# The norm's factor per token left out of the second block's operand and given to the results, with the operand turned during the down projection

## What is computed

```python
def hybrid_layer(x, cos, sin, norm_g, w_in, gate_bias, conv_w, ...):
    h = rms_norm_2(x, norm_g)              # x * rsqrt(mean(x^2) + eps) per token, times g per channel
    proj = jnp.einsum('bsd,dn->bsn', h, w_in)
    (q_a, k_a, v_a, o_a, i_a, f_a, z_a, c_q, c_kv, k_r, z_b, g_a, g_b) = jnp.split(proj, offsets, axis=-1)
    qk_a = jax.nn.silu(causal_depthwise_conv(jnp.concatenate([q_a, k_a], axis=-1), conv_w))
    q_a, k_a = jnp.split(qk_a, 2, axis=-1)
    h_a = mlstm_chunkwise(q_a, k_a, v_a, i_a + gate_bias[:H_A], f_a + gate_bias[H_A:])
    y_a = einsum(sigmoid(o_a) * rms_norm_2(h_a, mlstm_norm_g) * silu(z_a), w_a)
    q_b  = einsum(rms_norm_2(c_q, q_lat_g), w_uq)
    kv_b = einsum(rms_norm_2(c_kv, kv_lat_g), w_ukv)
    ...                                     # head norms, rotation of k_r and of part of q_b, causal attention o_b
    y_b = einsum(o_b * silu(z_b), w_b)
    return x + einsum(sigmoid(g_a) * y_a + sigmoid(g_b) * y_b, w_out)
```

## Time and profile before

| | |
|---|---|
| median of 3 runs | 2552.49 us (2551.92 to 2555.49) |
| the profiled execution's own time | 2552.33 us |
| its span in the trace | 2550.3 us |
| PE busy | 2511.5 us, 98% |
| PEld busy | 2131.9 us, 84% |
| DVE busy | 1619.7 us, 64% |
| ACT busy | 1251.4 us, 49% |
| POOL busy | 143.7 us, 6% |
| mean rate from memory | 200 GB/s |

### The profile page before, as it was taken

How to read it: one execution, slowest core, us unless ns; L and a number is a source line. 1 busy time by engine, 2 the same in 40 slices (tenths; PEclk the granted TensorE clock), 3 DMA queues, 4 the chain that set the end, 5 groups by cost and what they waited for, 6 DMA issues and landing times.

```text
span 2550.3 us, 34507 instructions
## 1 busy us (share of the span) xinstructions
PE 2511.5 (98%) x13608; PEld 2131.9 (84%) x13608; DVE 1619.7 (64%) x2365; ACT 1251.4 (49%) x1899; POOL 143.7 (6%) x148
## 2 busy tenths in 40 slices
PE   6999999999999999999999999999999999999999
PEld 2689899998888888888888888988888888888887
DVE  3566787786588886566665666665555554545554
ACT  3244433334465554355554555555566665544443
POOL 1001100000001110001110000001000000000000
PEclk9999999999999999999999999999999999999999
DMA  9953777775569885566665455555554555555555
GB/s 335 333 182 112 233 245 249 244 240 183 206 193 273 266 261 191 193 189 189 191 189 192 163 169 174 174 170 184 174 164 150 157 166 189 181 190 183 189 189 165
DMA packets 459104, 511.42 MB, mean 201 GB/s; under 512 B 36771, under 2 KB 327682, under 8 KB 458432
## 3 DMA queue, kind: packets, MB, share of 16 engines
q1 hardware_dynamic: 455936, 501.11, 62.0%
q0 software_dynamic: 2864, 8.11, 1.0%
q10 hardware_dynamic: 144, 0.02, 0.0%
HBM read 506.93 MB, written 2.22 MB: 200 GB/s over the span
## 4 chain that ended last, share of the span: by engine, by line
PE 94%; ACT 2%; DVE 2%; SPq 1%; issue 1%; DMA 0%; DVEq 0%; ACTq 0%
PE PG L926 17%; PE PG L928 17%; PE PG L927 17%; PE PG L916 13%; PE PG L919 6%; PE PG L935 4%; PE PG L937 4%; PE PG L936 4%; PE PS L1040 1%; SPq L746 1%; PE PS L831 1%; ACT wh L1179 1%; PE PG L847 1%; PE PS L1104 1%; PE PG L849 1%
## 5 line engine op out<-in xcount | busy, mean ns | idle before, releaser
L1576 DVE TENSOR_TENSOR wl<-raw,wh 128x1024 fp32r<-128x1024 f32 (+1 forms) x745 | 911.3, 1227 | 702.7 <-ACT wh L1179 701.0
L1179 ACT ACTIVATE wh<-raw 128x1024 fp32r<-128x1024 f32 (+1 forms) x745 | 786.7, 1058 | 860.7 <-PE PG L928 574.8
L916 PE MATMUL PG<-FHL,wh 128*128 128x512 f32 x1376 | 430.8, 396 | 2.4 <-DVE UP L1832 1.5
L926 PE MATMUL PG<-wh,HHL 128*128 128x512 f32 x832 | 331.2, 398 | 0.1
L928 PE MATMUL PG<-wl,HHL 128*128 128x512 f32 x832 | 324.8, 390 | 0.0
L927 PE MATMUL PG<-wh,HHL 128*128 128x512 f32 x832 | 324.1, 390 | 0.0
L919 PEld LDWEIGHTS PG<-FHL,wl 128*128 128x128 f32 x1376 | 256.2, 188 | 59.6
L919 PE MATMUL PG<-FHL,wl 128*128 128x256 f32 x1376 | 267.9, 278 | 0.0
L916 PEld LDWEIGHTS PG<-FHL,wh 128*128 128x128 f32 x1376 | 210.8, 189 | 5.2 <-issue 3.7
L928 PEld LDWEIGHTS PG<-wl,HHL 128*128 128x128 f32 x832 | 156.1, 188 | 33.6
L927 PEld LDWEIGHTS PG<-wh,HHL 128*128 128x128 f32 x832 | 156.5, 188 | 30.7
(11 more groups left out here) (402 smaller groups left out, 4213.0 us busy)
## 6 DMA issues: line engine op xcount, KB each, us to landing
raw<-in_w_in SPq DMA_DIRECT2D x208, 512.0 KB, 3.4
raw<-in_w_up SPq DMA_DIRECT2D x344, 256.0 KB, 3.4
raw<-in_w_ada SPq DMA_DIRECT2D x128, 512.0 KB, 5.0
raw<-in_w_down SPq DMA_DIRECT2D x84, 512.0 KB, 3.6
raw<-in_w_qkv SPq DMA_DIRECT2D x80, 512.0 KB, 4.4
first<-in_w_ada SPq DMA_DIRECT2D x78, 256.0 KB, 6.7
...
```

The source lines that it names most:

```text
L916: pe.matmul(to, hi[:, 128 * j:128 * j + 128], flat(FHL[:, step.k, :, :]), start=step.first, stop=False, skip_group_check=True)
L926: pe.matmul(dst, xh[:, cols], hi, start=step.first and j % per == 0, stop=False, skip_group_check=True)
L1179: ac.activation(wh[n % NSPL][:, 0:src.shape[1]], src, ACT.Copy).then_inc(S["hi"], 1)
L1576: dv.tensor_tensor(wl[n % NSPL][:, 0:x], src, wh[n % NSPL][:, 0:x], ALU.subtract).then_inc(S["lo"], 1)
```

## The change

The operand `HHL` of the second block is now made of XT, the residual itself, times g2; the factor per token `xr` is left out and multiplied into each product's result. With that, no transpose has to wait for the norm:

- `warm` and `scale` are gone for "h". The groups i = 0 to 5 of `turned` stand in `down1` (group i in column group i//2 + 1, at steps 5 and 8), groups 6 and 7 at steps 3 and 6 of lat.
- `norm` for "h" stands at step 1 of lat. A new job `rows_h` makes the factor also as rows: at step 2 DVE multiplies the identity with xr (DIAGH), at step 4 PE multiplies a matrix of ones with DIAGH, which gives the factor of each token in every partition, and at step 5 ACT copies that to RR.
- Results with tokens on the partitions get `scale=xr` in the ACT instruction that reads them. A scale column holds for 128 tokens, so what was one instruction of 128x1024 becomes two of 128x512 (mv_out, sig, silu, out, mix, mixb). lat's squares get xr too, and `lr` is multiplied by it.
- Results with tokens along the row are multiplied by RR on DVE: KRF and the two gate rows from small (the bias comes in two further instructions, and ACT's copy to KRF is gone), and all of mqk by a new instruction per product, MSG = PG times RR, 128x1024, at step 0 of the mv product. ACT's centre tap and DVE's other taps read MSG.
- Apart from this, the pair g = 1 of the first block's attention gets other steps for some of its pieces.

```diff
@@ -307,7 +307,7 @@
...
         if g == 1:
-            after, plus = ("k", 2, 0), ((14, 15, 16, 17, 18, 19, 25, 25, 26, 26), (27, 27, 28, 28, 29, 30, 32, 32, 33, 34))
+            after, plus = ("k", 2, 0), ((14, 15, 16, 17, 18, 19, 27, 27, 29, 29), (27, 28, 29, 29, 30, 31, 33, 33, 34, 35))
         if g == 7:
...
@@ -361,8 +361,13 @@
...
-    normed("h", ("tail2", 0, 0), ("lat", 0, 0))
+    P.put(("lat", 0, 0), 1, "norm", "h", 0)
+    for phase, n in enumerate((2, 4, 5)):
+        P.put(("lat", 0, 0), n, "rows_h", 0, phase, phase == 1)
+    for i in range(8):
+        turned("xh", i, ("down1", i // 2 + 1, 0) if i < 6 else ("lat", 0, 0), (5 if i < 6 else 3) + 3 * (i % 2))
...
@@ -375,6 +380,7 @@
...
     for g in range(4):
+        P.put(("mv", g, 0), 0, "m_conv", g, 6)
         P.put(("mv", g, 0), 0, "m_conv", g, 0)
...
@@ -581,6 +587,10 @@
...
+    DIAGH = at("DIAGH", [128, 2, 128], F32, 178)
+    RR = at("RR", [128, T], F32, 179)
+    MSG = [at(f"MSG{i}", [128, 4, T], F32, 140 + 4 * i) for i in range(2)]
...
@@ -606,7 +616,7 @@
...
-        return emptied(u + k) if k < 2 else emptied(u)
+        return emptied(u + k) if z == "f" and k < 2 else emptied(u)
...
@@ -690,7 +700,7 @@
...
-             "xf": (HN["f"], FHL[:, :, :, :].rearrange("p k a t -> p a k t"), "f", A1[:, 0, :]), "xh": (HN["h"], HHL, "h", g2)}
+             "xf": (HN["f"], FHL[:, :, :, :].rearrange("p k a t -> p a k t"), "f", A1[:, 0, :]), "xh": (XT, HHL, "h", g2)}
...
@@ -1004,13 +1014,17 @@
...
-                p = P.of["up" if key == "f" else "lat", 0]
+                p = P.of["up", 0]
...
+            elif (job, phase) == ("rows_h", 1):
+                w.wait_ge(S["diag_h"], 1)
+                w.wait_ge(*free(u))
+                pe.matmul(ps[:, 0:T], ones[:, :], flat(DIAGH[:, :, :]), start=True, stop=True).then_inc(S["side"], 1)
...
@@ -1087,13 +1101,15 @@
...
-                elif name in ("xf", "xh"):
+                elif name == "xf":
...
-                        w.wait_ge(S[f"scaled{n}"], nth("scale", (name[1], i), 0))
+                        w.wait_ge(S[f"scaled{n}"], nth("scale", ("f", i), 0))
+                elif name == "xh":
+                    w.wait_ge(S["res"], 2 * nth("res", ("down1", i // 2), 0))
...
-                apart = name in ("xf", "xh") and i == 0
+                apart = name == "xf" and i == 0
...
@@ -1324,9 +1340,10 @@
...
-            elif (job, phase) == ("small", 0):
-                w.wait_ge(*product_done("small", 0))
-                ac.activation(KRF[:, :], result("small", 0)[0:64, 0, 0:T], ACT.Copy).then_inc(S["kr_raw"], 1)
+            elif (job, phase) == ("rows_h", 2):
+                u = use("rows_h", 0, 1)
+                w.wait_ge(*full(u))
+                ac.activation(RR[:, :], bank(u)[:, 0:T], ACT.Copy).then_inc(emptying(u), 1)
...
@@ -1344,10 +1361,11 @@
...
                 w.wait_ge(*product_done("lat", key))
+                w.wait_ge(S["xr"], 2)
                 if key == 1:
...
                 for n in range(2):
-                    end = ac.activation(LJUNK[:, n, :], result("lat", key)[:, n, :], ACT.Square,
+                    end = ac.activation(LJUNK[:, n, :], result("lat", key)[:, n, :], ACT.Square, scale=xr[:, n:n + 1],
                                         accum_out=lss[:, 2 * key + n:2 * key + n + 1])
...
@@ -1360,23 +1378,24 @@
...
-                w.wait_ge(*product_done("mqk", g))
+                w.wait_ge(*out_done("mqk", g))
...
-                    end = ac.activation(MQK[b][:, j, :], result("mqk", g)[:, j // 2, T * (j % 2):T * (j % 2) + T],
-                                        ACT.Identity, scale=cw2[:, 3, ch:ch + 1])
+                    end = ac.activation(MQK[b][:, j, :], MSG[b][:, j, :], ACT.Identity, scale=cw2[:, 3, ch:ch + 1])
...
-                w.wait_ge(*out_done("mqk", key))
+                w.wait_ge(S["m_taps"], key + 1)
...
-                ac.activation(MV[key % 2][:, :, :, 0:T], result("mv", key)[:, :, :].rearrange("p j (h e) -> p j h e", h=2),
-                              ACT.Copy).then_inc(out_sem("mv", key), 1)
+                for n in range(2):
+                    end = ac.activation(MV[key % 2][:, n, :, 0:T], result("mv", key)[:, n, :].rearrange("p (h e) -> p h e", h=2),
+                                        ACT.Copy, scale=xr[:, n:n + 1])
+                end.then_inc(out_sem("mv", key), 1)
...
@@ -1406,15 +1425,19 @@
...
                     w.wait_ge(S["gated"], n - 1)
-                ac.activation(RG[n % 2][:, :, :], result(name, g)[:, :, :],
-                              ACT.Sigmoid if name == "sig" else ACT.Silu).then_inc(out_sem(name, g), 1)
+                for j in range(2):
+                    end = ac.activation(RG[n % 2][:, j, :], result(name, g)[:, j, :],
+                                        ACT.Sigmoid if name == "sig" else ACT.Silu, scale=xr[:, j:j + 1])
+                end.then_inc(out_sem(name, g), 1)
             elif (job, phase) == ("mix", 0):
...
                     w.wait_ge(*full(use("turned", ("ha", 7), 0)))
-                ac.activation(cols4(GA if name == "mix" else GB, g), result(name, g)[:, :, :],
-                              ACT.Sigmoid).then_inc(out_sem(name, g), 1)
+                for j in range(2):
+                    end = ac.activation(cols4(GA if name == "mix" else GB, g)[:, j, :], result(name, g)[:, j, :],
+                                        ACT.Sigmoid, scale=xr[:, j:j + 1])
+                end.then_inc(out_sem(name, g), 1)
             elif (job, phase) == ("qr_out", 0):
...
@@ -1892,10 +1914,26 @@
...
-                dv.tensor_scalar(gates[:, 0, :], ps[64:72, 0, 0:T], gb[:, 0:1], None, ALU.add)
-                w.wait_ge(S["kr_raw"], 1)
-                dv.tensor_scalar(gates[:, 1, :], ps[96:104, 0, 0:T], gb[:, 1:2], None,
-                                 ALU.add).then_inc(out_sem("small", 0), 1)
+                w.wait_ge(*product_done("small", 0))
+                w.wait_ge(*emptied(use("rows_h", 0, 1)))
+                dv.tensor_tensor(KRF[:, :], ps[0:64, 0, 0:T], RR[0:64, :], ALU.mult).then_inc(S["kr_raw"], 1)
+                dv.tensor_tensor(gates[:, 0, :], ps[64:72, 0, 0:T], RR[64:72, :], ALU.mult)
+                dv.tensor_tensor(gates[:, 1, :], ps[96:104, 0, 0:T], RR[96:104, :], ALU.mult).then_inc(c.sem, c.up())
+                w.wait_ge(c.sem, c.n)
+                dv.tensor_scalar(gates[:, 0, :], gates[:, 0, :], gb[:, 0:1], None, ALU.add)
+                dv.tensor_scalar(gates[:, 1, :], gates[:, 1, :], gb[:, 1:2], None, ALU.add).then_inc(out_sem("small", 0), 1)
+            elif (job, phase) == ("rows_h", 0):
+                w.wait_ge(S["xr"], 2)
+                dv.tensor_tensor(DIAGH[:, :, :], ident[:, :].unsqueeze(1).to_broadcast([128, 2, 128]),
+                                 xr[:, :].unsqueeze(2).to_broadcast([128, 2, 128]), ALU.mult).then_inc(S["diag_h"], 1)
+            elif (job, phase) == ("m_conv", 6):
+                g, b = key, key % 2
+                w.wait_ge(*product_done("mqk", g))
+                w.wait_ge(*emptied(use("rows_h", 0, 1)))
+                if g >= 2:
+                    w.wait_ge(S["m_centre"], g - 1)
+                dv.tensor_tensor(MSG[b][:, :, :], result("mqk", g)[:, :, :].rearrange("p a (c n) -> p (a c) n", c=2),
+                                 RR[:, :].unsqueeze(1).to_broadcast([128, 4, T]), ALU.mult).then_inc(out_sem("mqk", g), 1)
...
@@ -1933,18 +1971,19 @@
...
-                dv.tensor_copy(lr[:, 2 * key:2 * key + 2], y).then_inc(S["lat_r"], 1)
+                dv.tensor_tensor(lr[:, 2 * key:2 * key + 2], y, xr[:, :], ALU.mult).then_inc(S["lat_r"], 1)
...
+                w.wait_ge(*out_done("mqk", g))
...
-                        out=MQK[b][:, j, d:T], in0=result("mqk", g)[:, j // 2, T * (j % 2):T * (j % 2) + T - d],
+                        out=MQK[b][:, j, d:T], in0=MSG[b][:, j, 0:T - d],
...
-                        end.then_inc(out_sem("mqk", g), 1)
+                        end.then_inc(S["m_taps"], 1)
...
```

More of the change, by code:

```diff
@@ L1506, in piece @@
                 w.wait_ge(*full(u))
-                if name in ("xf", "xh") and i == 0:
-                    if name == "xf":
-                        w.wait_ge(S["gain"], NCH + 1)
+                if name == "xf" and i == 0:
+                    w.wait_ge(S["gain"], NCH + 1)
                     for k in range(2):
```

22 lines of the change are left out of this document (9 added, 13 removed).

## The result

| | before | changed |
|---|---|---|
| median | 2552.49 us (5 runs, 2551.92 to 2555.49) | 2563.33 us (5 runs, 2562.64 to 2564.0) |
| profiled execution | 2552.33 us | 2563.46 us |
| span | 2550.3 us | 2561.7 us |

The changed kernel is slower: the ratio to the kernel before is 1.004, with a 95% interval of 1.0029 to 1.0052. The medians lie 10.8 us apart, where 5.9 were forecast. The direction and the waits came as forecast; that TensorE's clock fell behind two of them did not. The measured time is 0.3 us above the top of the range.

The account below looks back on a forecast made before the run. PE, busy 98% of the span, was taken to bound the kernel. The terms summed as 2552.33 - 4.2 + 0.1 + 9.3 + 1.5 - 0.7 = 2558.3, with 0.16 to the median 2558.4 us; range 2548.5 to 2563.0.

Parts of the forecast that it names:

- Opening of lat: Between down projection and lat: 9.02 us without product removed, less transposes and waits for a low part and DIAGH; net gain 4.2.
- small: PE's transposes of KRF wait 0.55 for DVE, the gate chain gets 0.1 longer, the next wait shrinks 0.45; net +0.1 us.
- Convolution: mv products: MSG delays the chain, PE waits 2.64 us for MP three times and 1.4 for a low part; +9.3 us.
- The clock rival: TensorE's clock falls behind four new waits of 2.4 to 2.6 us, costing 6.9 us: 2565.3 us; chance 0.07.
- signs of being wrong: Listed trace findings, such as no wait for MP or one above 3.5 us, or granted clock under 1.00 behind a wait.
- Shorter taps: Convolution taps on DVE, reading SBUF instead of PSUM, get 65 ns shorter each: 2556.1 us; chance 0.05.
- Halves: ACT readers split into two 128x512 instructions, 0.25 us more each, on the path six times in the MLA part: +1.5 us.
- Attention: First block's attention: moved pieces of two heads shorten PE's single wait of 2.46 us for PT; -0.7 us.

Follow-up runs that it names:

- Run 4: Changed kernel with the last squares, the norm and the factor's rows moved to later steps of lat: 2559.86 us.
- Run 1: Changed kernel without the multiply MSG on mqk's results, centre tap and taps reading the accumulator again: 2549.45 us.
- run 2: Changed kernel with ten matmuls nobody reads put ahead of PE's wait for MP, for heads 1, 3 and 5: 2559.52 us.
- Run 8: Kernel before the change, without the 28 matmuls nobody reads between the two blocks: 2555.94 us.
- run 3: Changed kernel with the convolution's taps moved behind MP, to steps 5 to 8, and silu to step 9: 2566.48 us.
- run 6: Changed kernel with readers of mv, sig, silu, out, mix and mixb as one 128x1024 instruction each, without the factor: 2562.68 us.
- run 7: Changed kernel with the first block's attention steps for pair g = 1 put back as before: 2564.87 us.

## Why the prediction was right, and where its size was off

- **Opening of lat.** Forecast -4.2, measured -4.1. The waits came as named: for the third tile's low part 0.60 in the list (forecast 0.89), for DIAGH 2.17 (2.44). PE also loses time as it starts again; counted from the product matmul ahead to the second one behind, the low part cost 0.87 besides its transposes, and DIAGH with its matmul 2.88, where 2.87 was forecast (2.44 and 0.43). A group of transposes costs 0.44 and not 0.35: I had read it from the start of the first matmul behind a group, and the second is later still (0.32 behind the first instead of 0.23). In the working, 1447.79 and 1.06 give 1448.85, not 1448.76; the 0.09 is the overlap of two instructions on ACT, which the changed trace has too, and was not said. Run 4 shows that both waits were a matter of place.
- **small.** Forecast +0.1, measured +0.6. KRF's wait is 0.48 (0.55). The step that failed is the offset against the next wait: I let it shrink by 0.45; in the changed trace it is 0.85 where it was 1.01, so the gate chain became longer by about 0.3 on DVE and not by 0.1, with five instructions for two. That shrinking by 0.16 lies in the table's row of mv 0, so the term as I had defined it came to about 0.4.
- **Convolution.** The term was +9.3. Its waits alone are right: 1.2 for the low part in mv 0, and 2.54, 2.53 and 2.56 for MP, each forecast at 2.64; with what is lost as PE starts again, 10.0 (1.5 and three times 2.8). The wrong step is that the term ended there. It measured 12.9, since each such wait can bring the lower clock behind it. Run 1 takes all of it away with one instruction, and run 2 parts it into waits and clock.
- **The clock rival.** I gave it 0.07, against a price of 6.9 us for four falls; two fell, for 3 us. A granted clock under 1.00 behind a wait was one of my signs of being wrong, and it came: what failed is to put at nothing what a wait does to the clock. The argument against it was one row: a wait of 2.46 with the clock at 1.00 behind it. Run 8 has a wait at the same place (2.9 us) with the clock at 0.57. One trace shows one throw. The trace of before had a row for the other side as well, which I passed over, PE's wait of 2.67 us near 60 us:

```profile
63.16 0.80 PE L847 MATMUL PG<-XHL,wh 128*128 128x512 f32 x1 [2.67 <-DVE wl L1576]
```

with, in its window,

```profile
63.00:67.00 4.00, 3.84 (x10) 3.06 (x11) 1.24 (x2) 0.28 (x1) 0.00 (x0) 0.58 1.10 351
```

All eleven traces have this wait, and in seven the clock fell behind it. Of the twelve waits for MP in the four traces that have them at full length, eight had the lower clock behind them; of the three for a low part in run 3 (2.0 to 2.1 us), all three; of the seven waits for DIAGH (2.2 us), one; of the three for PT, one. The Trainium skill's advice (TensorE: Matmul & The Clock Gate, "Why this matters for your kernels") is to avoid idle gaps above about 3 us. The measurement decides against reading that as a safe side: the clock fell here behind gaps of 2.0 to 2.7 us.

- **Shorter taps.** The rival is refuted directly. In the changed kernel a tap from SBUF (L1982) takes 482 ns, one from PG took 481, where the table of the Trainium skill (VectorE: DVE Perf Modes, "The TRN2 errata — SBUF-src ops pay a fixed extra latency per instruction") would, by my estimate from it, have had 65 less. The measurement decides.
- **Halves.** Forecast +1.5, measured +1.25, and 1.4 in the trace of run 6.
- **Attention.** Forecast -0.7, measured -0.3, which run 7 repeats with 0.34.
- **Range.** It ended at 2563.0, because the clock case was left out of it. With its two falls at 3 us added to the forecast the sum is 2561.4; of the other 2, about 1.5 are the sizes of small (0.5), the convolution's restarts (0.7), attention (0.4) and the opening (0.1), less 0.25 of the halves; the rest is no more than the start-up's scatter between executions.
